# First attention of a two-block layer stack on half tiles of the TensorE array, with an input that arrives in pieces

## What is computed

```
qkv = rms_norm(x, mixer_norm) @ w_qkv
q, k = rope(rms_norm(q, q_norm)), rope(rms_norm(k, k_norm))       # per head, 64 columns
scores = q @ k.T / 8, masked to kj > qi and kj <= qi + 128        # blocks of 128 rows
m = maximum(scores.max(-1), sink)
p = exp(scores - m)
probs = p / (p.sum(-1) + exp(sink - m))
x = x + (probs @ v) @ w_o
```

## Time and profile before

| | |
|---|---|
| Median of 3 runs | 2513.69 us (2513.17 to 2515.67) |
| The profiled execution's own time | 2515.65 us |
| Its span in the profile | 2513.5 us |
| TensorE busy | 2468.9 us, 98% |
| VectorE busy | 1806.8 us, 72% |
| ScalarE busy | 1174.8 us, 47% |
| Mean granted TensorE clock | 0.995 of 2.4 GHz |
| DMA | 577.10 MB, mean 230 GB/s |

### The profile page before, as it was taken

The page is one execution under the profiler, slowest core; times in us unless marked ns, Lnnn a source line. Parts: engine busy times, 40 slices in busy tenths (PEclk is TensorE's granted clock), DMA queues, the critical chain, the costliest instruction groups (busy, mean ns, idle before and its releaser), DMA issues.

```text
span 2513.5 us, 31043 instructions
## 1 busy us (share of the span) xinstructions
PE 2468.9 (98%) x11359; PEld 2033.3 (81%) x11359; DVE 1806.8 (72%) x2444; ACT 1174.8 (47%) x1575; POOL 41.4 (2%) x62
## 2 busy tenths in 40 slices
PE   7999999999999999999999999999999989999998
PEld 6888888888888888788888888888888778888886
DVE  6655678787777777577787777778776676666655
ACT  5565544444443444454444444444444454455553
POOL 1100000000000000000000000000000000000000
PEclk9999999999999999999999999999999999999999
DMA  7333688888888887467777787777777547776653
GB/s 258 123 110 112 213 288 280 294 286 297 289 286 284 299 281 265 141 204 235 241 229 234 226 265 244 245 225 242 230 233 240 152 147 250 249 234 216 223 189 125
DMA packets 159765, 577.10 MB, mean 230 GB/s; under 512 B 18016, under 2 KB 18272, under 8 KB 159616
## 3 DMA queue, kind: packets, MB, share of 16 engines
q1 hardware_dynamic: 157648, 570.80, 69.2%
q0 software_dynamic: 816, 2.23, 0.3%
q10 hardware_dynamic: 1152, 2.10, 0.2%
HBM read 572.96 MB, written 2.10 MB: 229 GB/s over the span
## 4 chain that ended last, share of the span: by engine, by line
PE 91%; DVE 4%; ACT 2%; issue 1%; DMA 1%; SPq 0%; POOL 0%; DVEq 0%; ACTq 0%
PE PS L942 28%; PE PS L944 28%; PE PS L943 28%; PE PS L548 2%; DVE WL L1891 1%; DMA AR<-in_pos 1%; ACT WH L1302 1%; ACT AR L1094 0%; PE PS L624 0%; PE PS L648 0%; DVE AR L1411 0%; ACT SQ L977 0%; DVE YA L1572 0%; PE PS L900 0%; PE PS L901 0%
## 5 line engine op out<-in xcount | busy, mean ns | idle before, releaser
L1891 DVE TENSOR_TENSOR WL<-W,WH 128x1024 fp32r<-128x1024 f32 x816 | 992.3, 1223 | 524.3 <-ACT WH L1302 516.6
L1302 ACT ACTIVATE WH<-W 128x1024 fp32r<-128x1024 f32 x816 | 857.1, 1059 | 862.3 <-PE PS L944 851.6
L942 PE MATMUL PS<-WH,XTH 128*128 128x512 f32 x2144 | 861.0, 402 | 15.2 <-DVE XTL L1391 9.8
L944 PE MATMUL PS<-WH,XTL 128*128 128x512 f32 x2144 | 838.6, 391 | 0.0
L943 PE MATMUL PS<-WL,XTH 128*128 128x512 f32 x2144 | 837.2, 390 | 0.0
L942 PEld LDWEIGHTS PS<-WH,XTH 128*128 128x128 f32 x2144 | 403.8, 188 | 100.3 <-issue 15.5
L944 PEld LDWEIGHTS PS<-WH,XTL 128*128 128x128 f32 x2144 | 403.2, 188 | 85.9
L943 PEld LDWEIGHTS PS<-WL,XTH 128*128 128x128 f32 x2144 | 404.2, 189 | 82.5 <-issue 3.8
L942 PE MATMUL PS<-WH,YTH 128*128 128x512 f32 x1120 | 443.4, 396 | 8.4 <-DVE YTL L1424 4.5
L944 PE MATMUL PS<-WH,YTL 128*128 128x512 f32 x1120 | 437.6, 391 | 0.0
L943 PE MATMUL PS<-WL,YTH 128*128 128x512 f32 x1120 | 437.0, 390 | 0.0
(11 more groups left out here) (272 smaller groups left out, 1274.7 us busy)
## 6 DMA issues: line engine op xcount, KB each, us to landing
W<-in_ada SPq DMA_DIRECT2D x192, 512.0 KB, 4.5
W<-in_avoz SPq DMA_DIRECT2D x192, 512.0 KB, 4.6
W<-in_wg SPq DMA_DIRECT2D x88, 512.0 KB, 4.9
W<-in_wu SPq DMA_DIRECT2D x88, 512.0 KB, 4.7
W<-in_wd SPq DMA_DIRECT2D x88, 512.0 KB, 4.8
W<-in_kada SPq DMA_DIRECT2D x64, 512.0 KB, 4.6
W<-in_aqk SPq DMA_DIRECT2D x64, 512.0 KB, 4.7
W<-in_aout SPq DMA_DIRECT2D x64, 512.0 KB, 4.4
```

The costliest lines, as they stand in the source:

```text
L942: e.matmul(p, x, WH[:, g % NH, j], start=first, stop=False)
L944: i = e.matmul(p, y, WH[:, g % NH, j], start=False, stop=last)
L1302: e.activation(WH[:, n % NH], W[:, i % NW], ACT.Copy).then_inc(s_hi, 1)
L1891: e.tensor_tensor(l, src, h.bitcast(F32), ALU.subtract).then_inc(s_lo, 1)
```

## The change

- The attention works on 12 pairs (`PAIRS`), three per key/value head: all eight heads of t = 0, then two times four heads of t = 1. Even heads lie in the lower, odd heads in the upper 64 rows. Scores are matmuls on 64 rows, alternating between rows 0 to 63 (into one bank) and rows 64 to 127 (into another), with keys K2 in place of KE and KO.
- No mask matmul: VectorE does scale, mask and maximum in one operation per head, from PSUM to SBUF, where ScalarE takes the exponential in place.
- VectorE divides the probabilities by their sum before they are turned. The product then has V as the loaded operand (64 columns) and the turned probabilities as the moving one (256 or 512 columns), even heads into partitions 0 to 63 and odd heads into 64 to 127 of one bank. It comes out turned, so `out_T` goes.
- `attention_steps` replaces `attention_order`: a pair begins at least 5 ticks (the last two 4) behind the one before, once q is ready, and each stage lies at a fixed tick: score 0, VectorE 1, exponential 3, division 6, turn 8, copy 9, product 11, YTH 12, YTL 13.
- q's two halves go through rope in consecutive ticks; k's sums and rope are made before the norm's statistics, which move behind unit 9.
- `outproj` for w_o: cuts at 4 and 6, only k = 7 last, no empty ticks; each unit waits for its own pairs alone.
- Start: ScalarE issues only the first xt; the other seven stand between the weight tiles on SyncE's queue. Of cols, the first 32 columns come first, the rest behind the fourth weight tile with rows and positions, and `rotary` waits for them too. X comes in eight pieces behind the sixth tile. The first eight units are converted one at a time.

The core of the diff ("..." marks what is left out, removed lines of more than four in a row too):

```diff
--- before.py
+++ after.py
-UNITS = [(0, (0, 1, 2, 3)), (0, (4, 5, 6, 7)), (1, (0, 1)), (1, (2, 3)), (1, (4, 5)), (1, (6, 7))]
+YT_ATT, YT_FFN, YT_MIX, YT_KV, YT_BAND = 0, (12, 20, 28), (34, 42), 50, 58
+
+PAIRS = [(0, 0, 4), (1, 0, 2), (1, 2, 2)]
+STEP_END = 13
...
@@ -180,7 +182,7 @@
         p = gs = 0
         for g in range(slots):
             lo = p
-            while p < len(stream) and (gs <= g + LOOK or p not in self.slot):
+            while p < len(stream) and (gs <= g + (LOOK if g >= 8 else 0) or p not in self.slot):
                 gs += p in self.slot
                 p += 1
             self.batch.append(range(lo, p))
...
-    def outproj(name, ver, nk, out, cut=(), pauses=0, after=({}, {})):
+    def outproj(name, ver, nk, out, cut=(), tail=2, after=({}, {})):
         pars = [at["chunk"] % 2, (at["chunk"] + 1) % 2]
         at["chunk"] += 2
-        n0 = nk - 2
+        n0 = nk - tail
         edges = (0,) + cut + (n0,)
         for a, b in zip(edges, edges[1:]):
             for c in (0, 1):
                 for k in range(a, b):
                     yield from unit(name, k, pars[c], k == 0, False, ver, True)
-        for _ in range(pauses):
-            yield ("tick",)
         for c in (0, 1):
             for k in range(n0, nk):
                 yield from unit(name, k, pars[c], False, k == nk - 1, ver, True)
...
@@ -235,21 +235,20 @@
         return (at["chunk"] - 1) % 2, at["g"]
 
     yield ("turn", 0, 0, 0)
-    yield ("turn", 0, 1, 0)
-    after = {k: [("turn", 0, k + 2, 0)] for k in range(6)}
+    after = {k: [("turn", 0, k + 1, 0)] for k in range(7)}
     after[0].append(("start", "rotary"))
-    for c in range(4):
-        after[c + 1].append(("square_in", c))
-    after[6] = [("stats", 0)]
+    after[7] = [("square_in", 3)]
+    for c, k in enumerate((3, 5, 6)):
+        after[k].append(("square_in", c))
     yield from chunk("X", 0, True, after=after)
     yield ("start", "kv") + last()
     for g in range(4):
-        yield from chunk("X", 0)
+        yield from chunk("X", 0, after={1: [("stats", 0)]} if g == 0 else {})
         yield ("start", "attn_q", g) + last()
         if g == 0:
             yield ("start", "attn_all")
     turn = [("turn", 1, k, at["g"]) for k in range(8)]
-    yield from outproj("Y0", YT_ATT, 8, "wo", cut=(4,), pauses=4,
+    yield from outproj("Y0", YT_ATT, 8, "wo", cut=(4, 6), tail=1,
                        after=({1: turn[0:1], 3: turn[1:2], 5: turn[2:3], 7: turn[3:4]},
                               {2: turn[4:5], 5: turn[5:6]}))
 
...
+def attention_steps(qready, at):
+
+    begun = []
+    k = 0
+    while len(begun) < 12 or k <= begun[-1] + STEP_END:
+        P = len(begun)
+        if P < 12 and (not begun or k >= begun[-1] + (5 if P < 10 else 4)) and (P // 3, PAIRS[P % 3][0]) in qready:
+            begun.append(k)
+        for P, k0 in enumerate(begun):
+            if k - k0 in at:
+                at[k - k0](P)
         k += 1
         yield
 
...
-                def score_(N):
-                    g, (t, hs) = N // 6, UNITS[N % 6]
+                def score_(P):
+                    g, (t, j0, n) = P // 3, PAIRS[P % 3]
                     k = 128 * (1 + t)
-                    b, full = take(("s", N))
+                    banks = [take(("s", P, a)) for a in range(2)]
                     w.wait_ge(s_qt, 2 * g + t + 1)
                     w.wait_ge(s_k, 2)
-                    w.wait_ge(s_kz, 1)
+                    for x in range(n):
+                        for a, (b, full) in enumerate(banks):
+                            h = slice(64 * a, 64 * a + 64)
+                            i = e.matmul(b[:, k * x:k * x + k], QT[h, t, j0 + x], K2[h, g, 0:k], start=True, stop=True)
+                            if x == n - 1:
+                                i.then_inc(full, 1)
+                    for a in range(2):
+                        give(("s", P, a), s_sm, 2 * P + a + 1)
+
+                def turn(P):
+                    t, _, n = PAIRS[P % 3]
+                    w.wait_ge(s_pn, P + 1)
+                    for a in range(2):
+                        b, full = take(("p", P, a))
+                        for x in range(4):
+                            f = x if t == 0 else 2 * (x % 2) + x // 2
+                            src = PB[P % 2][:, 512 * a + 128 * f:512 * a + 128 * f + 128]
+                            i = e.transpose(b[:, 128 * x:128 * x + 128], src, ident[:])
+                        i.then_inc(full, 1)
+                        give(("p", P, a), s_pt, 2 * P + a + 1)
+
+                def pv(P):
+                    g, (t, j0, n) = P // 3, PAIRS[P % 3]
+                    b, _ = take(("o", P), False)
+                    w.wait_ge(s_pt, 2 * P + 2)
                     w.wait_ge(s_v1, 2)
...
+                    m = 128 * n
+                    for k in range(1 + t):
+                        for a in range(2):
+                            i = e.matmul(b[64 * a:64 * a + 64, 0:m], V1[:, k, 64 * g:64 * g + 64],
...
+                yield from attention_steps(qready, {3: score_, 9: turn, 12: pv})
 
...
                                      ACT.Copy).then_inc(s_hi, 1)
 
-            for k in range(8):
-                e.dma_start(XS[:, 2 * k:2 * k + 2].rearrange("p a k -> p (a k)"), A["xt"][k]).then_inc(s_x[k], 16)
+            e.dma_start(xs(0), A["xt"][0]).then_inc(s_x[0], 16)
...
@@ -1457,6 +1426,7 @@
             def rotary():
                 w.wait_ge(s_pos, 16)
                 w.wait_ge(s_rows, 16)
+                w.wait_ge(s_cols, 16)
                 settle()
...
-                    e.tensor_scalar(sm(u, 3), sm(u, 2), r8[:, t:t + 1], None, ALU.mult)
-                    e.tensor_scalar(sm(u, 4), sm(u, 2), r8n[:, t:t + 1], None, ALU.mult).then_inc(s_qs, 1)
+
+                turned(0)
+                yield
+                turned(1)
+                yield from ticks(4)
+                for t in range(2):
+                    u = 4 * t + g
+                    w.wait_ge(s_hr, 2 + 2 * g + t + 1)
+                    e.tensor_scalar(sm(u, 3).rearrange("p (a j) -> p a j", a=2),
+                                    sm(u, 2).rearrange("p (j a) -> p a j", a=2), r8[:, t:t + 1], None,
+                                    ALU.mult).then_inc(s_qs, 1)
...
+                    return rows[:, RS + 8 * g:RS + 8 * g + 8].rearrange("p (j a) -> p a j", a=2)[:, :, j0:j0 + n]
+
+                def score_(P):
+                    g, (t, j0, n) = P // 3, PAIRS[P % 3]
                     k, u = 128 * (1 + t), 4 * t + g
-                    nh, h0 = len(hs), hs[0]
-                    mx, ng = sm(u, 5)[:, h0:h0 + nh], sm(u, 6)[:, h0:h0 + nh]
-                    b = full(("s", N))
-                    step(e.tensor_reduce(mx, b[:, :].rearrange("p (a k) -> p a k", k=k), AX.X, ALU.max))
+                    w.wait_ge(s_qs, 2 * g + t + 1)
+                    w.wait_ge(s_const, N_CONST)
+                    if P >= 2:
+                        w.wait_ge(*filled(("p", P - 2, 1)))
+                    for a in range(2):
+                        b = full(("s", P, a))
+                        for x in range(n):
+                            h = 4 * a + j0 + x
+                            i = e.tensor_tensor_reduce(PB[P % 2][:, 512 * a + k * x:512 * a + k * x + k],
+                                                       b[:, k * x:k * x + k], mrow[:, 128 - 128 * t:256],
+                                                       sm(u, 3)[:, h:h + 1], rows[:, RS + 8 * g + 2 * (j0 + x) + a:
+                                                                                  RS + 8 * g + 2 * (j0 + x) + a + 1],
+                                                       ALU.add, ALU.max, sm(u, 5)[:, h:h + 1])
+                        i.then_inc(s_sm, 1)
+                    w.wait_ge(s_sm, 2 * P + 2)
+                    e.tensor_scalar(pair(u, 6, j0, n), pair(u, 5, j0, n), -1.0, None, ALU.mult).then_inc(s_ng, 1)
+                    w.wait_ge(s_ng, P + 1)
+                    e.tensor_tensor(pair(u, 8, j0, n), pair(u, 6, j0, n), sinks(g, j0, n), ALU.add).then_inc(s_sk1, 1)
+
+                def scale(P):
+                    g, (t, j0, n) = P // 3, PAIRS[P % 3]
+                    k, u = 128 * (1 + t), 4 * t + g
+                    w.wait_ge(s_p, P + 1)
+                    w.wait_ge(s_sk2, P + 1)
+                    step(e.tensor_tensor(pair(u, 10, j0, n), pair(u, 9, j0, n), pair(u, 7, j0, n), ALU.add))
                     settle()
-                    w.wait_ge(s_qs, 2 * g + t + 1)
-                    step(e.tensor_tensor(ng, mx, sm(u, 4)[:, h0:h0 + nh], ALU.mult))
+                    step(e.reciprocal(pair(u, 11, j0, n), pair(u, 10, j0, n)))
                     settle()
...
-                                    b[:, :].rearrange("p (h d) -> p h d", d=64),
-                                    sm(u, 11).unsqueeze(2).to_broadcast([128, 8, 64]), ALU.mult).then_inc(s_ao, 1)
-                    tasks.start(out_T(g, t))
-
...
```

(14 more changed lines are left out.)

292 lines of the change are left out of this document (105 added, 187 removed).

## The result

The changed kernel takes 2505.62 us (median of 11 runs, 2501.31 to 2510.22); the kernel before, on the same chips, 2515.67 us (11 runs, 2513.17 to 2517.70). The ratio is 0.9962, with an interval of 0.9953 to 0.9972: some 10 us less. That is faster by more than the 0.2% that can be told apart, and inside the stated range of 2476 to 2506 by 0.4 us, but little more than a third of the 27 us forecast. The profiled execution took 2504.3 us.

A forecast was written before the change was run, and what follows sets the result against it. TensorE, busy 98% of the span, was taken to bound the kernel. Start 7 + attention 20 + waits 0 = 27 us off the profiled 2515.65 gives 2488.7, as median 2487; range 2476 to 2506.

The forecast's parts named there:

- TensorE's attention work: Attention stretch: twelve pairs in place of 24 units cut TensorE's work from 68.3 to 48.0 us, 20 us less.
- overlapped end of the two bounds: Scores and products on half tiles: side by side 48.0 us in all, against 67.2 us if not overlapped.
- Rival 1: Attention's half tiles take turns without overlap, so the gain is 1 + 7 = 8 us: 2506; chance 0.15.
- The start's marks: Start: first matmul near 7.7 us, positions landed near 13, unit 2 near 17.5, unit 7 near 34.5.
- One to one to the end: TensorE is busy every microsecond from 296.5 to 1000 us, so a microsecond saved earlier should come off the end.
- TensorE's waits in the stretch: Attention stretch: TensorE's idle time stays at 6.6 us, with bounds 0 and 20, adding 0 to the sum.
- The last x tile and all X pieces: Start, SyncE's queue: these transfers stand behind waits for a conversion but are wanted only units later.
- My bound of 3 for the start: Start: lower bound of the 7 us gain, only the first matmul's shift; the upper bound was 10.
- The price of the fused operation: VectorE in attention: 64 multiply-add-and-max operations at 0.28 us (128 columns) and 0.42 us (256), 23 us.
- Rival 2: Attention: VectorE or the fixed distances bind, gain per chunk falls from about 5 to 2 us: 2499; chance 0.15.
- Rival 3: Attention: each pair holds TensorE over 2.3 us, waiting for normalised probabilities; at 3 us each, slower at 2523; chance 0.05.
- Rival 4: The start gives nothing, as rotary also waits for the columns and VectorE is late; attention as forecast: 2494; chance 0.10.

The follow-up runs named there:

- the changed kernel again: The changed kernel with no edit, measured again to see its scatter: 2505.46 us, ratio 0.9964 to the kernel before.
- the ropes apart: Changed kernel with last pairs' YTL a step earlier and X's last square a unit later, plus q's second half three ticks behind in rope: 2489.1 us.
- less work: Changed kernel with last pairs' YTL earlier and X's last square later, plus division of only two columns per head (output not the reference's): 2485.25 us.
- the later turn: Changed kernel with last pairs' YTL earlier and X's last square later, plus turn through output one step later for nine pairs: 2488.51 us.
- the best version here: Changed kernel with last pairs' YTL earlier, X's last square later, first nine pairs' turns one step later and q's ropes three ticks apart: 2485.68 us.

## Why the prediction was right in sign and 17 us off in size

Right, step by step:

- **TensorE's attention work.** Forecast 20 us less, measured 20.4. The overlapped end of the two bounds was the right one; the terms are within 0.2 us per group (scores and product 1.27 and 1.23 with the switch, forecast 1.0 + 0.35). Rival 1 (the halves take turns) is out. The Trainium skill, "TensorEngine Tiling (Array Packing)", Key Properties, has different tiles work in parallel; by that rule the sum is the 48.0 us, and this trace agrees, with 46.7.
- **The start's marks.** First matmul 7.44 (7.7 forecast), the rotary step at 13.77 (landing near 13), unit 2 at 18.34 (17.5), unit 7 at 34.96 (34.5).
- **One to one to the end.** The feed-forward part is full from its first matmul on. Past 1000 us another 2 us appear (1502.0 for what took 1503.9 before), but they can't be credited to the change: from the start of the feed-forward part to the end the profiles have 2216.7 us before, 2215.0 after, 2217.1 for the changed kernel again, and 2215.3 for the kernel before with the new start alone.

The measured time lies inside the stated range by luck: the forecast's own range was 2478 to 2496, and the upper end, 2506, was there for rival 1, the half tiles taking turns, which didn't happen.

Wrong, and the steps that failed:

1. **"TensorE's waits in the stretch ... I leave at 6.6."** They were 16.3 us, and the clock, for which the sum had no term, took 5.2 more. These 14.8 us are most of the miss. The step went wrong in three places. At the tail I had seen "one short wait": there are two, 2.0 and 2.8 us, and they are not short by themselves but closed in a circle, as YTL stands behind a conversion that waits for TensorE; one step earlier gave 5.6 us. In the middle I had compared sums, 29 us of VectorE in 33.5 of TensorE, and called 87% "hidden, but with little to spare". The sum was even nearly right (170.2 busy for a forecast of 156 + 11); the share says nothing of a turn that comes two steps behind a division, when rope and conversion lie between them. Later turn and spread ropes together gave 8.4 us. And banks: 4.6 of the 10.0 us at the turns end with YTL or the fused operation, which give back banks of PSUM; the prediction looked at the banks of the keys only.
2. **"The last x tile and all X pieces stand behind waits for a conversion; they are wanted units later."** The last piece is wanted right behind unit 7. It landed at 37.8, and 3.0 us of the 7 were lost there; squares one unit later gave 2.9. I had priced SyncE's issues and not followed the last piece to who waits for it. My bound of 3 for the start was the nearer value: 3.5 in this profile, and in the kernel with the new start alone nothing that the medians tell apart.
3. **The price of the fused operation.** Two of the four groups on VectorE between 40 and 288 us (the others take the same):

```profile
L1564 DVE CUSTOM_DVE_ANT_0 YA<-PS,mrow,AR 128x256 f32<-128x256 f32 x16 | 7.8, 542 | 0.0
...
L1564 DVE CUSTOM_DVE_ANT_0 AR<-PS,mrow,AR 128x128 f32<-128x128 f32 x16 | 5.5, 405 | 0.0
```

Forecast were 0.42 and 0.28 us. The operation with two scalars by pointer takes 0.54 and 0.405, 0.12 us more than plain operations of these widths (0.415, and 0.280 for 128 columns at line 1505 before); as the next one starts before it ends, 0.47 apart in the timeline for 256 columns, the 64 cost 26.5 us instead of 23. That is 3 of the 14 us that VectorE gained, a small term.

Rival 2 (VectorE or the fixed distances bind, 2499) named the mechanism of the waits for the division, and it is what happened; its price, 2 us of gain per chunk instead of 5, came near the 10 us lost to turns. It lacked the tail, the banks and the clock. Rival 3's wait, TensorE held at the normalised probabilities, exists too, at 5.4 us over twelve pairs, under 0.5 us each on average where the change would have turned slower above 2.3. Rival 4 (the start gives nothing) was half true: half of the forecast 7 us in the changed kernel, none that can be told apart with the old attention.

Open stays why the clock falls behind some waits and not behind others: in the profile of the changed kernel the turns at 139.10 and 153.34 us waited for 2.63 and 2.14 us and the matmuls behind them came at full pace, while behind the one at 177.24, which waited for 1.39, they were 0.43 us apart from 179.7 to 182.4. The places also differ from run to run (the changed kernel's runs span 8.9 us, those of before 4.5). The clock was not separated from the waits before it. In single profiles the ropes apart took 4.5 us of idle time away at an unchanged clock, and the time fell by 5.0; with less work and with the later turn the clock rose too.

## What to carry to other kernels

A fixed distance between stages has to be checked against the queue of each engine in its worst stretch (what stands between the two stages in program order, and what each of these waits for), not against its mean load, and against the step that gives back the buffer which the stage needs; and where an instruction that a consumer wants stands behind one that waits for that consumer, it has to move ahead, however short it is. When transfers are reordered, follow the last piece through the waits of its queue to the instruction that reads it, and then look at what is queued behind that reader. A saving on the bounding engine comes only as far as the others keep up: the best version here took the changed kernel from 10 us of gain to 29.5 with nothing but moved steps.

## What the runs showed of the hardware

- Float32 matmuls on 64 rows, or into 64 columns, of different halves ran side by side at the full array's pace, 0.216 us per 256 columns each, and did so even when the upper half's stood four records behind the lower half's in the program. The Trainium skill, "TensorEngine Tiling (Array Packing)", Key Properties, has tiles compute in parallel; that the order of the two halves in the program didn't matter (2505.51 against 2505.46 us) is what the runs add. Entering and leaving the shape cost about 0.3 us per group: 1.27 and 1.23 us counted from the weight matmul ahead, against 0.91 for the same stream on the whole array (line 648 before).
- Waits of 1.4 to 3.4 us within dense work were in some places followed by weight matmuls 0.43 us apart instead of 0.227, at the lower of the two levels (granted clock 0.50), for about 3 us or more; others of 2.1 and 2.6 us weren't. Eleven runs of the changed kernel, with 16 us of waits in the stretch, span 8.9 us, and eleven of the kernel before, with 6.6, span 4.5.
- A fused multiply-add-and-maximum that reads two scalars by pointer took 0.54 us for 256 columns from PSUM, where a plain operation takes 0.415.
